# Decoder trunk: first section by half blocks, zeros between, first loads from three queues

## What is computed

```python
D_MODEL, SEQ, DEPTH, D_FF = 1024, 256, 2, 2816
def swiglu_ffn(x, w_in, w_out):
    gate, up = jnp.split(x @ w_in, 2, axis=-1)
    return (jax.nn.silu(gate) * up) @ w_out

for l in range(DEPTH):
    h = layer_norm(ALPHA * h + 0.5 * swiglu_ffn(h, ffn_w_in[l, 0], ffn_w_out[l, 0]), ...)
    h = layer_norm(ALPHA * h + hybrid_mixer(h, w_in[l], w_o[l], ...), ...)
    h = layer_norm(ALPHA * h + 0.5 * swiglu_ffn(h, ffn_w_in[l, 1], ffn_w_out[l, 1]), ...)
```

## Time and profile before

| | us |
|---|---|
| median of 3 runs | 968.86 |
| lowest, highest | 968.77, 970.0 |
| the profiled execution | 969.25 |
| its span, first to last instruction | 967.3 |
| PE busy | 956.5 (99% of the span) |
| DVE busy | 659.3 (68%) |
| ACT busy | 508.1 (53%) |
| POOL busy | 37.0 (4%) |

### The profile page before, as it was taken

One profiled execution on the slowest core, in us unless ns is written; L12 is line 12 of the kernel. 1 busy time (PEld: TensorE's weight loads), 2 busy tenths in 40 slices (PEclk: granted clock), 3 DMA queues, 4 the chain that ended last, 5 costly groups with the idle time before them and its releaser, 6 DMA issues.

```text
span 967.3 us, 14780 instructions
## 1 busy us (share of the span) xinstructions
PE 956.5 (99%) x5295; PEld 813.7 (84%) x5295; DVE 659.3 (68%) x954; ACT 508.1 (53%) x688; POOL 37.0 (4%) x43
## 2 busy tenths in 40 slices
PE   8999999999999999999999999999999999999997
PEld 5888888889877888888888888888988788888886
DVE  5665655689998565655676565567999876565555
ACT  5554545455674545545455554544557655554541
POOL 0000000011002000000010000002000010000000
PEclk9999999999999999999999999999999999999999
DMA  9756556567325756557555655565763355655551
GB/s 307 248 175 213 178 189 236 193 219 220 132 88 159 233 173 198 192 177 239 170 196 174 210 180 185 199 224 177 240 210 115 122 194 178 195 194 177 194 195 43
DMA packets 124642, 182.32 MB, mean 188 GB/s; under 512 B 6080, under 2 KB 98368, under 8 KB 123840
## 3 DMA queue, kind: packets, MB, share of 16 engines
q1 hardware_dynamic: 123552, 178.91, 56.3%
q0 software_dynamic: 912, 2.88, 1.1%
q10 hardware_dynamic: 144, 0.07, 0.0%
HBM read 178.69 MB, written 1.05 MB: 186 GB/s over the span
## 4 chain that ended last, share of the span: by engine, by line
PE 98%; DVE 1%; DMA 1%; SPq 0%; issue 0%; ACT 0%; DVEq 0%
PE bank L537 30%; PE bank L541 16%; PE ybank L503 10%; PE ybank L509 10%; PE ybank L507 10%; PE bank L476 2%; PE ybank L746 2%; PE ybank L750 2%; PE ybank L751 2%; PE bank L479 2%; PE bank L483 2%; PE bank L430 2%; PE bank L665 1%; PE bank L733 1%; PE ybank L476 1%; PE ybank L479 1%
## 5 line engine op out<-in xcount | busy, mean ns | idle before, releaser
L1108 DVE TENSOR_TENSOR w_lo<-raw,w_hi 128x2048 fp32r<-128x2048 f32 (+1 forms) x155 | 355.1, 2291 | 238.0 <-ACT w_hi L884 238.0
L537 PE MATMUL bank<-xT,w_hi 128*128 128x512 f32 x1280 | 446.3, 392 | 0.0
L884 ACT ACTIVATE w_hi<-raw 128x2048 fp32r<-128x2048 f32 x160 | 305.7, 1911 | 258.0 <-PE bank L541 112.1
L541 PE MATMUL bank<-xT,w_lo 128*128 128x256 f32 x1280 | 359.5, 281 | 0.0
L537 PEld LDWEIGHTS bank<-xT,w_hi 128*128 128x128 f32 x1280 | 240.3, 188 | 52.6
L541 PEld LDWEIGHTS bank<-xT,w_lo 128*128 128x128 f32 x1280 | 240.8, 188 | 1.6
L503 PE MATMUL ybank<-w_hi,yT_hi 128*128 128x512 f32 x416 | 165.9, 399 | 0.3
L509 PE MATMUL ybank<-w_hi,yT_lo 128*128 128x512 f32 x416 | 162.8, 391 | 0.0
L507 PE MATMUL ybank<-w_lo,yT_hi 128*128 128x512 f32 x416 | 162.0, 389 | 0.0
L503 PEld LDWEIGHTS ybank<-w_hi,yT_hi 128*128 128x128 f32 x416 | 78.2, 188 | 18.2 <-issue 2.6
L509 PEld LDWEIGHTS ybank<-w_hi,yT_lo 128*128 128x128 f32 x416 | 77.9, 187 | 18.4
(11 more groups left out here) (127 smaller groups left out, 855.3 us busy)
## 6 DMA issues: line engine op xcount, KB each, us to landing
raw<-in_ffn_in SPq DMA_DIRECT2D x172, 512.0 KB, 4.7
raw<-in_ffn_out SPq DMA_DIRECT2D x88, 512.0 KB, 3.9
raw<-in_w_in SPq DMA_DIRECT2D x40, 512.0 KB, 4.5
raw<-in_w_o SPq DMA_DIRECT2D x16, 512.0 KB, 4.1
gb<-in_ln_gb SPq DMA_DIRECT2D x6, 1024.0 KB, 7.1
raw<-in_w_in SPq DMA_DIRECT2D x4, 520.0 KB, 6.3
raw<-in_ffn_in SPq DMA_DIRECT2D x8, 256.0 KB, 6.0
qk_swap<-qk_raw POOLq DMA_DIRECT2D x16, 128.0 KB, 3.0
```

The source lines that it names most:

```text
L537: m = eng.matmul(dst[:, :], wh[:, k, g, cols], xT[:, kk, :, :].rearrange("p a n -> p (a n)"), start=kk == 0, stop=False, skip_group_check= ...
L541: m = eng.matmul(dst[:, SEQ:2 * SEQ], wl[:, k, g, cols], xT_hi[:, kk, :], start=False, stop=kk == KT - 1, skip_group_check=True)
L884: eng.activation(w_hi[:, s, 0:width], raw[:, s, 0:width], ACT.Copy).then_inc(hi_done, 1)
L1108: eng.tensor_tensor(w_lo[:, s, 0:width], raw[:, s, 0:width], w_hi[:, s, 0:width].bitcast(F32), ALU.subtract).then_inc(lo_done, 1)
```

## The change

Five things are changed, all in the first section and the start.

1. Order of the first section. SP loads x half (0,0), half (1,0), unit 0's pieces 1 to 3, x half (0,1), unit 1's piece 0, x half (1,1), unit 1's pieces 1 to 3 (in the names (t,h), t is the tile and h the half). PE transposes (0,0), then after unit 0's first piece for tile 0 (1,0), and (0,1) and (1,1) around the products of unit 0's piece 3. Each piece is used for both tiles before the next one. ACT and DVE follow. PE waits for `x_loaded` itself, without POOL's count between.
2. Unit 2 too is loaded, copied and split in four pieces, ahead of both `silu`; unit 3 comes after both.
3. Three more matmuls on zeros stand behind the first four transposes.
4. The first piece of unit 0 is loaded by ACT's queue instead of SP's.
5. The identity is loaded by POOL's queue, ahead of its memset, instead of ACT's.

The counts that follow from this are adjusted (`slot_load`, `unit_used`, and the first load of the second chunk's units outside the loop).

```diff
+            for u in range(2):
+                load_x(0, u)
+                if u > 0:
+                    load_piece(u, 0)
+                load_x(1, u)
+                for k in range(1, 4):
+                    load_piece(u, k)
+            for k in range(4):
+                load_piece(2, k)
...
-            def first_pieces():
-
-                for t in range(T):
-                    stage_x(0, 0, t)
-                    m = pieces(0, t)
-                m.then_inc(unit_used, 1)
-                for t in range(T):
-                    pieces(1, t).then_inc(gu_done, 1)
...
+            def first_T(t, h):
+
+                if h > 0:
+                    eng.wait_ge(xT_ready, t + 1)
+                eng.wait_ge(x_loaded[2 * t + h], 16)
+                transposes(bank[2 + t], [xn[:, t, (4 * h + k) * P:(4 * h + k + 1) * P] for k in range(4)])\
+                    .then_inc(xT_psum, 1)
...
+            def first_pieces():
+
+                first_T(0, 0)
+                zero_products(3)
+                piece(0, 0, 0, (1, 0))
+                piece(0, 0, 1)
+                piece(0, 1, 0)
+                piece(0, 1, 1)
+                piece(0, 2, 0)
+                piece(0, 2, 1)
+                first_T(0, 1)
+                piece(0, 3, 0)
+                first_T(1, 1)
+                piece(0, 3, 1).then_inc(unit_used, 1)
                 for k in range(4):
...
+                    for t in range(T):
+                        m = piece(1, k, t)
+                        if k == 3:
+                            m.then_inc(gu_done, 1)
...
-            eng.dma_start(cst[:, 0:EARLY], consts[:, 0:EARLY]).then_inc(cst_loaded, 16)
+            first = ffn_in[0, 0].rearrange("(k p) (g n) -> p k g n", p=P, g=2)
+            eng.dma_start(raw[:, 0, 0:BANK].rearrange("p (g n) -> p g n", g=2), first[:, 0, :, 0:CHUNK])\
+               .then_inc(piece_loaded[0], 16)
             eng.wait_ge(pool_setup, 1)
...
+            eng.dma_start(cst[:, 0:EARLY], consts[:, 0:EARLY]).then_inc(cst_loaded, 16)
             eng.memset(minus_half[:, :], -0.5).then_inc(pool_setup, 1)
```

More of the change, by code:

```diff
@@ L278, in trunk @@
         x_loaded = [sem(f"x_loaded{n}") for n in range(T * HALVES)]
-        piece_loaded = [sem(f"piece_loaded{n}") for n in range(8)]
+        piece_loaded = [sem(f"piece_loaded{n}") for n in range(12)]
         piece_hi = sem("piece_hi")
@@ new lines, in piece @@
+            def piece(u, k, t, between=None):
+                kk, cols, tok = 4 * u + k, slice(k * BANK, (k + 1) * BANK), slice(t * P, (t + 1) * P)
+                eng.wait_ge(xT_hi_done, 2 * u + t + 1)
+                wait_piece(piece_hi, hi_done, u, k)
+                eng.matmul(bank[t][:, :], xT_hi[:, kk, tok], w_hi[:, u, cols], start=kk == 0, stop=False)
+                eng.wait_ge(xT_ready, 2 * u + t + 1)
+                eng.matmul(bank[t][:, :], xT_lo[:, kk, tok], w_hi[:, u, cols], start=False, stop=False)
+                wait_piece(piece_lo, lo_done, u, k, RING)
+                m = eng.matmul(bank[t][:, :], xT_hi[:, kk, tok], w_lo[:, u, cols], start=False, stop=kk == KT - 1)
+                if between is not None:
+                    first_T(*between)
@@ L884, in split_hi, with piece_hi_part, first_hi @@
                 eng.activation(w_hi[:, s, 0:width], raw[:, s, 0:width], ACT.Copy).then_inc(hi_done, 1)
[L886 to L892, removed]
+            def piece_hi_part(u, k):
+                cols = slice(k * BANK, (k + 1) * BANK)
+                eng.wait_ge(piece_loaded[4 * u + k], 16)
+                eng.activation(w_hi[:, u, cols], raw[:, u, cols], ACT.Copy).then_inc(piece_hi if k < 3 else hi_done, 1)
+            def first_hi(t, h):
+                eng.wait_ge(xT_psum, 2 * h + t + 1)
+                eng.activation(xT_hi[:, 4 * h:4 * h + 4, t * P:(t + 1) * P],
+                               bank[2 + t][:, :].rearrange("p (k n) -> p k n", k=4), ACT.Copy).then_inc(xT_hi_done, 1)
             def stage_hi(l, j, tiles):
@@ L949, in ffn @@
                 first, last = l == w == 0, l == DEPTH - 1 and w == 1
-                stage_hi(l, 2 * w, (0,))
                 if first:
-                    pieces_hi(0)
-                    stage_hi(l, 2 * w, (1,))
[L954 to L960, removed]
+                    for u in range(2):
+                        first_hi(0, u)
+                        piece_hi_part(u, 0)
+                        first_hi(1, u)
+                        piece_hi_part(u, 1)
+                        piece_hi_part(u, 2)
+                        piece_hi_part(u, 3)
+                    for k in range(4):
+                        piece_hi_part(2, k)
+                    silu(l, f, 0, 0, 0)
+                    silu(l, f, 0, 1, 0)
+                    split_hi(l, b, 3)
+                else:
+                    stage_hi(l, 2 * w, (0,))
+                    split_hi(l, b, 2)
+                    stage_hi(l, 2 * w, (1,))
+                    silu(l, f, 0, 0, 0)
+                    split_hi(l, b, 3)
+                    silu(l, f, 0, 1, 0)
                 split_hi(l, b, 4)
@@ L1109, in split_lo, with piece_lo_part, first_lo @@
                                   ALU.subtract).then_inc(lo_done, 1)
[L1111 to L1120, removed]
+            def piece_lo_part(u, k):
+                cols = slice(k * BANK, (k + 1) * BANK)
+                if k < 3:
+                    eng.wait_ge(piece_hi, 3 * u + k + 1)
+                else:
+                    eng.wait_ge(hi_done, u + 1)
+                eng.tensor_tensor(w_lo[:, u, cols], raw[:, u, cols], w_hi[:, u, cols].bitcast(F32), ALU.subtract)\
+                   .then_inc(piece_lo if k < 3 else lo_done, 1)
+            def first_lo(t, h):
+                eng.wait_ge(xT_hi_done, 2 * h + t + 1)
+                part = (slice(None), slice(4 * h, 4 * h + 4), slice(t * P, (t + 1) * P))
+                eng.tensor_tensor(xT_lo[part], bank[2 + t][:, :].rearrange("p (k n) -> p k n", k=4),
+                                  xT_hi[part].bitcast(F32), ALU.subtract).then_inc(xT_ready, 1)
             def stage_lo(l, j, t):
@@ L1206, in ffn @@
                 if l == w == 0:
[L1207 to L1214, removed]
+                    for u in range(2):
+                        first_lo(0, u)
+                        piece_lo_part(u, 0)
+                        first_lo(1, u)
+                        piece_lo_part(u, 1)
+                        piece_lo_part(u, 2)
+                        piece_lo_part(u, 3)
+                    for k in range(4):
+                        piece_lo_part(2, k)
+                    gated(l, f, 0, 0, 0)
+                    gated(l, f, 0, 1, 0)
+                    split_lo(l, b, 3)
+                else:
+                    split_lo(l, b, 2)
+                    gated(l, f, 0, 0, 0)
+                    split_lo(l, b, 3)
+                    gated(l, f, 0, 1, 0)
                 split_lo(l, b, 4)
```

41 lines of the change are left out of this document (21 added, 20 removed).

## The result

The changed kernel takes 971.09 us (median of 14 runs, 969.59 to 972.99), the kernel before 969.11 beside it (14 runs, 968.77 to 970.0). The ratio is 1.002 (95% interval 1.0012 to 1.0027): slower by 2 us, at the edge of what 0.2% separates, and outside the range of 967.7 to 970.6. It also scatters over 3.4 us where before scatters over 1.2, which turned out to be the better clue.

What follows compares the result with a forecast made beforehand. TensorE, busy 99%, was taken as the bound, so only an earlier start of its unbroken run could pay. -0.44 for order plus 0.3 for the identity gave -0.15 us off the median 968.86: 968.7, range 967.7 to 970.6.

Steps and rivals of the forecast that it cites:

- Order of the first section: First section: the new order of copies, transposes and products starts the wide products at 21.07, 0.44 us earlier than before.
- Loads on SyncE: SyncE's queue at the start: no landing is on the path, and the 5.90 us transfer step leaves the chain.
- First weights by ScalarE: Unit 0's first piece: issued at 0.75, landed by 5.2 to 6.9, needed at 6.12; cost nothing, up to 0.7.
- Identity by GpSimd: Identity load ahead of the first transposes: issue 0.75, 4.0 us to landing, transposes 0.4 late; cost 0.3 (0 to 2.1).
- The first rival: Identity load: lands late on GpSimd's queue, deciding from about 5.1 on; +0.3 to +1.7 us (969.2 to 970.6), chance 0.2.
- The slow pace lasts: First products: late identity leaves PE idle, 10 to 15 products cost 0.43; +2 to +3, 970.9 to 972; chance 0.08.
- Signs of being wrong: Transposes starting after 5.4, 128x512 products past 8 us spaced 0.43, or a w_hi copy awaiting DMA after 6.5.
- The three zero products: Behind the first transposes: 0.7 to 1.3 us together, inside a 1.5 us wait, so cost nothing.
- After E: Second section: unit 3 split by 25.9, needed at E + 6.1 = 27.2, slack 1.2 us; cost nothing.

Runs made afterwards that it cites:

- the run with twelve zeros: Changed kernel with 12 zero products instead of 7 at the very start: 970.48 us, ratio 1.0016 to the kernel before.
- the old queues: Changed kernel with the identity loaded by ScalarE and all x and weights by SyncE again: 969.0 us, ratio 0.9999 to the kernel before.
- second profile: Changed kernel run again unchanged: 971.17 us, ratio 1.0024 to the kernel before; the profiled execution took 972.14.
- tile 1's transposes up front: Changed kernel, loads as before on ScalarE and SyncE, tile 1's first half block transposed right behind tile 0's, three zero products removed: 968.11 us, ratio 0.9987 to before.
- both queue edits: Kernel before, old order, with the identity issued by GpSimd and unit 0's first piece by ScalarE: 971.55 us, ratio 1.0024.
- the identity alone: Kernel before with only the identity's load moved to GpSimd, ahead of its memset: 970.44 us, ratio 1.0013.
- without the three zeros: Changed kernel, identity by ScalarE, all x and weights by SyncE, without the three zero products behind the first transposes: 970.34 us, ratio 1.0011 to before.
- the two runs with x first: As tile 1's transposes up front, but both half blocks of x loaded before weights: 967.95 us (0.9987); with five zero products behind the transposes 967.88 (0.9985).

## Why the prediction was wrong, step by step

Two of its terms failed, and both failures begin in the first 6 us: the identity's 0.3, which was mis-sized, and the pace, which the sum left at nothing. Of the 2.0 to 2.2 us that the change costs, 0.9 to 1.5 go to the late identity and 0.7 to 1.1 to the pace. The bounds come from two readings: the profiled execution of 970.0 stands 0.9 above the median of before and 1.1 below that of the change, and the run with twelve zeros 1.5 above before and 0.7 below the change.

- **Order of the first section: right.** Worked out 21.07 for the start of the wide products at a punctual identity, measured 21.15. The forecast gain of 0.44 was a difference to one slightly long execution of before; between medians it is zero (0.9999, interval 0.999 to 1.0008).
- **Loads on SyncE: right.** No weight piece and no x is in the chain of after.
- **First weights by ScalarE, "cost nothing": right in the change.** They landed at 5.1 (4.3 us from 0.76) and were first copied at 6.95. Behind the identity on the same queue the load took 5.9 us once, and PE waited for it.
- **Identity by GpSimd, "Cost 0.3": mis-sized.** I took the issue at 0.75 and 4.0 us to landing. GpSimd issued at 1.27 or 1.28 in every profile that has this load, after 0.82 idle that its own sequencer ended, and the landing took 4.4. Transposes 1.24 late, E (the start of the wide products) 0.9 later than with the old queues (22.07 against 21.15), and 1.3 later where the load took 4.9. The first rival had the right mechanism and its point of decision, 5.1, was passed in all profiles that have both new queues. The 0.4 us by which the first byte comes later on GpSimd's path by the Trainium skill ("DMA: Bandwidth & Descriptors", Specifications) did not cover it: 0.53 of later issue and 1.2 of longer landing (4.4 against 3.2) were measured with a second stream beside it, 0.2 of landing (3.4) without.
- **"The slow pace lasts", chance 0.08: the step that failed.** The sum has nothing for it. It costs 0.7 to 1.1 in the typical execution, and 2.1 where the rise came at 14.1 (24.21 against 22.07). The rival's own time, 970.9 to 972, holds the measured 971.09; the range left it out. The argument against it, "after the gap of 1.35 at 5.97 the products still ran at the fast pace", compared unlike gaps. That gap came after the first rise (the eight transposes of before take 1.45 us, all at the slow pace they take 1.97), this one ahead of or around it. And three other profiles show a fall after the rise, for which the rival had only the gaps near 9 us as a hint; in two of them the fall comes at those gaps.
- **Signs of being wrong.** Two that I had named came: first transposes after 5.4 (5.76), and products past 8 us with a spacing of 0.43 (second profile).
- **The three zero products, "cost nothing": right about their price, silent about their worth** (1.1 to 1.4 us in this order).
- **After E: right.** Unit 3 was split at 26.8 (24.49 and 4.49 for units 3 and 4 together), ahead of its use at E + 6.1, and the two spans differ by 0.57 where the starts of the second section differ by 0.56.
- **Range and chances.** I built the range from one profile each, and left the pace out of it. The scatter of single executions was the sign that more than one mechanism decided.

What stays open: why the pace rises late or falls in one execution of a kernel and not in the next, and holds over a gap of 1.67 us (tile 1's transposes up front); how much of the loss exactly is lateness and how much pace; what lies in the 0.1 to 0.4 us that some versions spend more outside their span; whether ScalarE's stream is what slows GpSimd's; and how the remaining difference between both queue edits (1.0024) and the identity alone (1.0013) divides, since the intervals touch.

## What to carry to other kernels

The first operand that everything waits for belongs on the queue that issues first and lands steadily; work out its landing from the issue time that the engine really reaches, not from the start of the program. At the head of a kernel, count TensorE's idle gaps as well as its lateness: waits of 0.6 to 1.8 us there cost some executions about 2 us more through the pace, and a few matmuls on zeros in waits that exist anyway took these executions away in three comparisons (scatter 3.0 to 1.1, 2.2 to 0.7 and 2.8 to 0.6 us). If a small edit widens the scatter of executions, take more than one profile, and read the distances between equal matmuls.

## What I had not expected of the hardware

- TensorE's pace can be up, fall and rise again within the first 13 us: without the three zeros the products of 6.88 to 9 us run at the fast pace, the granted clock is 0.53 from 9 to 12.5 and 0.98 to 1.00 after, with no idle time beyond 1.3 us in it.
- The same 64 KB load took 3.1 to 3.6 us from ScalarE's queue and 3.4 to 4.9 us from GpSimd's, and GpSimd began to issue it at 1.28 in all five profiles, 0.5 later than the other two engines their first loads.
- A load's place in SyncE's queue moves its landing by more than its issue: the same half block of x was issued at 1.91 in third place and landed at 6.93, after 5.0 us; in second place it was issued at 1.20 and landed after 3.6 and 3.3 us (the two runs with x first).
